# Fewer constant matmuls, later constants and an earlier output projection in a four-layer transformer kernel

## The reference

```
for layer in range(DEPTH):
    h = rms_norm_2(x, norm_g[layer])
    cols = split_columns(h @ w_in[layer])
    y_gdn = gdn_branch(cols, ...)
    y_mla = mla_branch(cols, positions, ...)
    y_rwkv = rwkv7_branch(cols, ...)
    mix = concatenate([y_gdn, y_mla, y_rwkv], axis=-1) * silu(cols['gate'])
    x = x + mix @ w_out[layer]
```

## Time and profile before

| | |
|---|---|
| median of three runs | 1312.51 us (1302.54, 1312.51, 1315.8) |
| the profiled execution: time | 1306.6 us |
| its span (first to last instruction) | 1304.5 us |
| PE busy | 1235.8 us, 95% |
| PE weight loads | 883.8 us, 68% |
| DVE busy | 755.2 us, 58% |
| ACT busy | 346.4 us, 27% |
| mean transfer rate | 114 GB/s |

### The profile page before, as it was taken

How to read it: one execution, slowest core, us unless ns; L and a number is a source line. 1 busy time by engine, 2 the same in 40 slices (tenths; PEclk the granted TensorE clock), 3 DMA queues, 4 the chain that set the end, 5 groups by cost and what they waited for, 6 DMA issues and landing times. The chain is left out here.

```text
span 1304.5 us, 18504 instructions
## 1 busy us (share of the span) xinstructions
PE 1235.8 (95%) x7285; PEld 883.8 (68%) x7285; DVE 755.2 (58%) x1471; ACT 346.4 (27%) x748; POOL 51.9 (4%) x92
## 2 busy tenths in 40 slices
PE   5999999999999998999999999999899999998997
PEld 5887649995446674599944478658567687575683
DVE  3154466765452145567743548884885279857872
ACT  2144321220012134121200132244351232434422
POOL 1100000000000000000000000200300000203000
PEclk9899899999999999999999999999999999999999
DMA  9532105544543431344445533220010433300000
GB/s 297 192 134 110 65 1 195 193 155 169 193 168 126 157 129 65 130 147 177 176 153 187 177 115 128 89 106 2 1 50 1 165 138 118 114 17 1 2 2 33
DMA packets 65854, 149.25 MB, mean 114 GB/s; under 512 B 2098, under 2 KB 8136, under 8 KB 65768
## 3 DMA queue, kind: packets, MB, share of 16 engines
q1 hardware_dynamic: 62432, 141.63, 30.7%
q0 software_dynamic: 1216, 3.52, 1.0%
q10 hardware_dynamic: 2119, 2.91, 0.9%
HBM read 146.95 MB, written 1.07 MB: 113 GB/s over the span
## 5 line engine op out<-in xcount | busy, mean ns | idle before, releaser
L1367 ACT ACTIVATE region<-banks 128x384 f32<-128x384 f32 (+8 forms) x159 | 77.1, 485 | 315.9 <-PE banks L443 106.3
L443 PE MATMUL banks<-hnT,weight_slabs 128*128 128x256 f32 x576 | 128.0, 383 | 3.4 <-DVE hnT L1843 3.4
L443 PEld LDWEIGHTS banks<-hnT,weight_slabs 128*128 128x128 f32 x576 | 109.8, 192 | 20.5 <-DVE hnT L1843 4.1
L495 PE MATMUL banks<-weight_slabs,region 128*128 128x512 f32 x256 | 115.1, 592 | 0.0
L495 PEld LDWEIGHTS banks<-weight_slabs,region 128*128 128x128 f32 x256 | 48.5, 190 | 60.3 <-issue 60.3
L495 PE MATMUL banks<-region 128*128 128x512 f32 x192 | 87.6, 592 | 0.0
L1826 DVE TENSOR_TENSOR region<-region 128x256 f32<-128x256 f32 (+23 forms) x160 | 75.7, 473 | 17.2 <-ACT region L1713 12.1
L1826 DVE TENSOR_TENSOR region<-weight_slabs 128x1024 f32<-128x1024 f32 x32 | 39.2, 1226 | 80.2 <-PE banks L495 76.4
L1984 DVE TENSOR_TENSOR region<-banks,region 128x128 f32<-128x128 f32 x40 | 11.7, 292 | 119.4 <-PE banks L610 94.1
L1826 DVE TENSOR_TENSOR region<-weight_slabs,region 128x1024 f32<-128x1024 f32 x64 | 78.2, 1222 | 1.1
L1323 POOL TENSOR_TENSOR region<-region,consts 128x240 f32<-128x240 f32 (+24 forms) x60 | 34.4, 599 | 966.1 <-DVEq L1835 945.2
(11 more groups left out here) (365 smaller groups left out, 2053.7 us busy)
## 6 DMA issues: line engine op xcount, KB each, us to landing
weight_slabs<-in_mlp_w SPq DMA_DIRECT2D x32, 2048.0 KB, 8.7
weight_slabs<-in_w_in SPq DMA_DIRECT2D x10, 2048.0 KB, 7.7
weight_slabs<-in_od_w_in SPq DMA_DIRECT2D x6, 2048.0 KB, 7.9
weight_slabs<-in_ev_w_in SPq DMA_DIRECT2D x4, 2048.0 KB, 11.9
weight_slabs<-in_w_out SPq DMA_DIRECT2D x4, 2048.0 KB, 7.8
weight_slabs<-in_ev_w_out SPq DMA_DIRECT2D x2, 2048.0 KB, 8.3
weight_slabs<-in_od_w_out SPq DMA_DIRECT2D x2, 2048.0 KB, 7.9
weight_slabs<-in_w_in SPq DMA_DIRECT2D x2, 2016.0 KB, 7.5
```

Of the source, the lines that this page charges most:

```text
L443: ins = mm(view(ps, b + i * S, (1, S)), view(slabs, o + k * width + c0, (1, P)), view(hnT, k * S, (1, S)), start=k == 0, stop=k == KC - 1)
L495: ins = mm(view(ps, b, (1, 512)), view(R, act + k * st, (1, P)), view(w, wt + k * step_, (1, 512)), start=n == 0 and k == 0, stop=n == 7 a ...
L1367: say(A(dst, view(ps, b, *(dims or ((1, n),)), np_=np_), ACT.Copy, scale=scale), read("scalar", *key))
```

## The change

Three edits:

1. SP no longer waits for `hn_ready` before the compression weights, and issues the constant array behind the q weights (entry 2) and ahead of the wait for entry 3.
2. The eight `warm` matmuls in the delta rule's inverse go, in layers 2 and 3: 16 matmuls, 32 records. All other `warm` calls stay.
3. In the attention of layer 1 the pieces of the output projection's first half start at i = 12 instead of 13 (3, 2, 3, 2, 2, 2 pieces at i = 12 to 17 for 3, 3, 2, 2, 2 at 13 to 17), and DVE adds tile (0,0) to `x` after head 14's logits and head 13's scaling instead of after the softmax.

```
@@ FILL[1]
-        {**{i: 5 for i in range(6)}, 6: 2, 7: 4, 8: 4, 9: 4, 10: 4, 13: 3, 14: 3, 15: 2, 16: 2, 17: 2})
+        {**{i: 5 for i in range(6)}, 6: 2, 7: 4, 8: 4, 9: 4, 10: 4, 12: 3, 13: 2, 14: 3, 15: 2, 16: 2, 17: 2})
@@ SP
                         sp.dma_start(dst, src).then_inc(*up("bucket_table_in", i, by=16))
+                if n == 3:
                     sp.dma_start(cst[:, C_ONE:C_EPS], a["const_masks"][:, C_ONE:C_EPS]).then_inc(*up("constants_in", 0, by=16))
-                if n == 1:
-                    sp.wait_ge(*at("hn_ready", "mix", 0, 0))
                 if n >= SLOTS:
@@ PE, mla_between
-                WARM = (("base", -1), ("base", 14), ("Z", 0), ("Y", 1), ("Z", 1), ("VT", 2), ("Z", 2), ("X", 2))
...
-                    if (what, n) in WARM:
-                        warm(1, "five")
@@ DVE
-            softmax(1, lambda name, h: h, lambda i: None, lambda i: moba_scale(i - 1) if i else None)
+            def after_1(i):
+                if i:
+                    moba_scale(i - 1)
+                if i == 14:
+                    residual(1, 0, TILES[:1])
+            softmax(1, lambda name, h: h, lambda i: None, after_1)
             moba_scale(15)
-            residual(1, 0, TILES)
+            residual(1, 0, TILES[1:])
```

## The result

| | before | changed |
|---|---|---|
| median | 1310.18 us of 6 (1302.54 to 1315.8) | 1327.15 us of 6 (1324.72 to 1330.97) |
| profiled execution, span | 1304.5 us | 1323.1 us |
| mean granted clock of PE | 0.986 | 0.956 |
| time at 1.2 GHz in the span | 36 us | 115 us |

The ratio of the times is 1.0137, 95% interval 1.0098 to 1.0177: the change costs 17 to 18 us. Forecast were 1302 us and a range that ends at 1312. In all six executions of the changed kernel the mean clock is 0.954 to 0.958, and in the 80 executions of the kernel before that ran beside the experiments it is 0.981 to 0.992: the two do not touch.

A forecast was written before the change was run, and what follows sets the result against it. PE's own instruction stream was taken to bound the kernel, busy 95% of the span. Gains of 5.9 + 4.7 + 0.2 less 3.0 gave 7.8 us, from 1309.4 to 1302 us, range 1293 to 1312.

The forecast's parts named there:

- the clock term of edit 2: Delta rule's inverses: without the repeats a longer wait lets the clock fall once per layer, 3 us lost, between 0 and 7.
- the last call: End of each inverse, ahead of the state's products: removing it gains nothing, since line 1236 waits for ACT's copy.
- the slower rival: Inverses of both layers: small matmuls run at the lower clock for most of their length; 1316 us, chance 0.08.
- the dense pieces stay in place, the twin did not fall: Argument against long low clock: dense lines 931, 1157, 1166 remain; layer 3's similar 2.85 us wait was followed by 1.00.
- Its sign of being wrong: Inverses: idle stretches turning into more than two clock falls a layer; also, at the start, the wait staying.
- the twins: Same program place: a 2.84 us wait in layer 2 preceded 3.41 us at 0.50; 2.85 us in layer 3 preceded 1.00.
- the rival of 1285 us: Inverses: the repeats were on PE's path, so all 13.8 us go and no clock falls; chance 0.08.
- The margin at the next bank: Layer 1 projection, tile (0,1) at i = 17: DVE frees the bank 0.2 us before PE needs it, so no wait.
- the 0.3 us added for what is not counted as idle: Layer 1 output projection: added to the 4.4 us of removed waits for uncounted time between rows, making 4.7 us.
- The order of transfers: Kernel start: constants behind the q weights let the q slab land sooner; PE goes on at about 29.8, gaining 2.5 us.
- SP's wait: Kernel start: removing SP's 5.0 us wait before issuing the compression weights was costed at nothing.
- The second term: Kernel start: with the standstill shortened, the 6.83 us at 0.50 behind it run at full clock, gaining 3.4 us.

The follow-up runs named there:

- Y 1 alone: Changed kernel with the constant matmul put back at one place per inverse, ahead of level Y 1: 1315.0 us, ratio 1.0049 to the kernel before.
- Y 1 and X 2: Changed kernel with one constant matmul put back at two of eight places, ahead of Y 1 and after X 2: 1301.45 us, ratio 0.9947 to before.
- edit 2 alone: Kernel before without the sixteen constant matmuls of the delta rule's inverses, nothing else changed: 1339.77 us, ratio 1.0233.
- edit 3 alone: Kernel before with only layer 1's output projection one step sooner and DVE's first addition inside the softmax: 1305.51 us, ratio 0.9945.
- edit 1 alone: Kernel before with only the constants issued behind the q weights and SP's wait for the normalized input gone: 1308.02 us, ratio 0.9975.
- small tiles: Changed kernel with twelve 64 x 64 matmuls of 32 columns at each of the eight places: 1309.15 us, ratio 0.9997 to the kernel before.

## Why the prediction was wrong

**The step that failed is the clock term of edit 2.** The prediction counted one fall per layer, of 3.41 us as in the earlier trace rows, at 1.5 us: 3 us, between 0 and 7. Measured are 30 us, as two long stretches per layer: 24 to 31 us from the levels Y on, which cost 7.0 and 8.6 us, and 17 us behind the state's products, which cost 7.6 us each. Two things were mis-sized in it.

- *The length.* All falls that ended within the span of before were 3.4 or 6.8 us long, and the prediction took the shorter for the length of a fall. None of them lay in the levels of the inverse; there the repeats kept the clock up. A length taken from the earlier trace rows was a length from another place.
- *The second place.* The wait at the state's products grew from 0.30 to 1.7 us. It is the repeat at X 2 that had kept it short: 1.35 us are idle with Y 1 alone, 0.30 with Y 1 and X 2. The prediction costed the last call at nothing, because the matmul behind it waits for ACT; it asked about the clock only at Y 1. What follows there is 17 us of PE's own work, where nothing hides a halved clock: 7.6 us a layer, half of the loss.

The mechanism was named, as the slower rival: the small matmuls at the lower clock for most of their length, deciding beyond 21.6 us at 1.2 GHz. It came at 89 us in the four stretches. It priced ten falls at 17 us and had a chance of 0.08; and its argument against (the dense pieces stay in place, the twin did not fall) was weak, for the earlier trace rows had one fall out of two such waits, and the change makes longer waits at three places (1.12, 2.71 and 1.70 us in layer 2). Its sign of being wrong counted falls, more than two a layer. In the levels and behind them there are just two a layer, and it is their length that costs. The rule of the page "TensorE: Matmul & The Clock Gate" of the Trainium skill, section "What's actually happening", that the prediction set beside the twins (the low clock is what PE has unless its activity lifts it) has these runs on its side: taking the filler out cost 2.3%. But that PE is busy is not enough to lift the clock here: it stayed at 1.2 GHz for 30.7 us with PE busy for 99.8% of them.

**The repeats themselves were hidden.** Right: from Y 1 to the state's products it is 20.9 us with them or without where the clock is 1.00, and the rival of 1285 us is out.

**Edit 3.** Right: 4.5 us between the rows named, against 4.7, and 0.9945 alone. The margin at the next bank, put at 0.2 us, held: DVE frees it at 514.4, and PE comes to it at 514.8. Of the 0.3 us added for what is not counted as idle, 0.1 came.

**Edit 1.** Right in one term of two. The order of transfers was right: the q slab landed 2.5 us sooner after its issue (12.0 to 9.5), and line 704 starts at 29.25 to 30.7 where 29.8 was forecast. SP's wait was worth nothing, as costed. The second term, 3.4 us for the low clock behind the wait, was taken from one execution as if it were in all, and as if nothing came in its place. With the same start, edit 2 alone has no fall there behind a wait of 1.55 us, and edit 3 alone has one of 10.2 us behind 2.13. With edit 1 alone it is gone, and the mean clock is still that of before: 0 of the 3.4 us. Alone, the edit gives 3.3 us (1.0 to 5.4), less than the 5.9; with edit 3 the two give 12.8 (9.7 to 16.1), where 10.6 were forecast.

**The sum.** 1309.4 - 10.6 + 30 = 1329, and 1327 was measured. With the right size of one term the sum stands, but partly by luck: edit 1 alone gave less than its term (3.3 against 5.9 us, which is outside its interval) and edit 3 alone more (7.2 against 4.7, within it).

## What to carry over

A matmul whose result nobody reads has its worth in the waits that it shortens, and so in the clock behind them: before it is removed, ask for each such wait what PE has to do behind it, and price all of that at 1.2 GHz, not the length of a fall that the trace shows elsewhere. A trace in which the clock is full because of such work can't show what its absence costs. The price is a cautious one: in layer 2, PE's busy time in the two stages is 20.4 and 14.1 us, the repeats included, so at half the clock throughout they would take up to 34.5 us more, and 14.6 were lost. It would still have warned, where 1.5 us a layer did not. And where two places matter of eight, the waits in the timeline without the filler name them, and putting it back at one place at a time shows what each is worth.

## What the runs showed that was not expected

- The clock stayed at 1.2 GHz for up to 30.7 us while PE was busy 99.8% of the time (30.63 of 30.70 us), in the levels of the inverse. A busy PE is not a sign of a full clock.
- It also stayed low for 17.1 us in five of six cases, and for 20.5 us in one, in a stream of PE's work without a gap (17.10 of 17.10 us busy) from the state's products on. The waits ahead of these were 1.70, 1.73 and 1.35 us; behind 0.85 us (small tiles) it was low for 13.7. Behind 0.30 and 0.64 us it was not low at all, but neither was it behind 1.19 us (small tiles, layer 2). So the length of a wait alone does not tell whether the clock falls.
- One constant 128 x 512 matmul (0.86 us) at two places a layer brings back 26 of 30 us; nearly the same PE time in 64 x 64 tiles, at all eight places, brings 18.
